# Neighbourhood attention on one core: the softmax reciprocal written 64 wide and transposed, scaling a step later, folds spread over 36 steps

## The reference

```python
# window: 8 rows x 16 columns of the token grid, clamped at the borders
s = jnp.einsum('bqhd,brqkhd->bqhrk', qi, kc) * scale + bias[None]
p = jax.nn.softmax(s.reshape(b, GRID_W, h, kh * WIN_COLS), axis=-1)
return jnp.einsum('bqhrk,brqkhd->bqhd', p, vc)
```

## Time and profile before

| | |
|---|---|
| median of 3 executions | 1835.57 us (1833.83 to 1836.62) |
| the profiled execution | 1836.12 us, its span 1834.1 us |
| granted TensorE clock, whole span | 0.984 of full speed |
| busy, share of the span | PE 97%, PEld 77%, DVE 46%, ACT 25%, POOL 28% |
| attention, 398 to 536 us: busy | PE 136.10, DVE 99.95, ACT 100.61, POOL 101.83 us |

### The profile page before, as it was taken

How to read it: one execution, slowest core, us unless ns; L and a number is a source line. 1 busy time by engine, 2 the same in 40 slices (tenths; PEclk the granted TensorE clock), 3 DMA queues, 4 the chain that set the end, 5 groups by cost and what they waited for, 6 DMA issues and landing times.

```text
span 1834.1 us, 22190 instructions
## 1 busy us (share of the span) xinstructions
PE 1779.0 (97%) x8481; PEld 1407.7 (77%) x8481; DVE 845.4 (46%) x1265; ACT 465.0 (25%) x803; POOL 521.3 (28%) x431
## 2 busy tenths in 40 slices
PE   7599999999999998899999999999999999999999
PEld 2466788877676886688888888888888888888887
DVE  2844588416876535524252615152433424252515
ACT  3533233227775004510101110111111111111010
POOL 0300122027854645005050505040312304050505
PEclk9799999999999999899999999999999999999999
DMA  9265101333323011011011110101010111101113
GB/s 344 92 195 181 37 23 35 67 73 72 76 72 136 24 35 41 17 35 35 24 35 34 34 34 15 42 23 46 23 46 23 34 34 34 34 23 34 34 34 137
DMA packets 107552, 108.70 MB, mean 59 GB/s; under 512 B 19463, under 2 KB 82145, under 8 KB 107241
## 3 DMA queue, kind: packets, MB, share of 16 engines
q1 hardware_dynamic: 106537, 104.82, 18.7%
q0 software_dynamic: 960, 3.15, 0.4%
HBM read 98.50 MB, written 9.45 MB: 59 GB/s over the span
## 4 chain that ended last, share of the span: by engine, by line
PE 75%; DVE 2%; issue 0%; ACT 0%; POOL 0%; DVEq 0%; ACTq 0%; POOLq 0%
PE banks L104 22%; PE banks L105 22%; PE banks L106 22%; PE banks L1006 2%; PE banks L1015 2%; PE banks L1345 2%; PE banks L1040 2%; PE banks L1024 1%; PE banks L992 1%; DVE h_hi L1701 0%; PE banks L1814 0%; DVE xn L1694 0%; DVE h_lo L1704 0%; PE banks L1328 0%; ACT t_second L1585 0%
## 5 line engine op out<-in xcount | busy, mean ns | idle before, releaser
L1768 POOL TENSOR_TENSOR x<-x,ff_scratch 128x512 f32<-128x512 f32 x198 | 263.4, 1364 | 834.5 <-DVE ff_scratch L1661 833.8
L104 PE MATMUL banks<-h_hi,wff_hi 128*128 128x512 f32 x1056 | 414.0, 392 | 10.9 <-POOL h_lo L1755 6.1
L105 PE MATMUL banks<-h_lo,wff_hi 128*128 128x512 f32 x1056 | 412.0, 390 | 0.0
L106 PE MATMUL banks<-h_hi,wff_lo 128*128 128x512 f32 x1056 | 411.9, 390 | 0.0
L1520 DVE TENSOR_TENSOR wff_lo<-wff_raw,wff_hi 128x1024 fp32r<-128x1024 f32 x66 | 81.5, 1235 | 404.3 <-ACT wff_hi L1516 404.3
L104 PEld LDWEIGHTS banks<-h_hi,wff_hi 128*128 128x128 f32 x1056 | 199.1, 189 | 52.0 <-issue 9.3
L106 PEld LDWEIGHTS banks<-h_hi,wff_lo 128*128 128x128 f32 x1056 | 198.9, 188 | 41.6
L105 PEld LDWEIGHTS banks<-h_lo,wff_hi 128*128 128x128 f32 x1056 | 199.1, 189 | 40.6
L1661 DVE TENSOR_TENSOR ff_scratch<-banks,gate 128x512 f32<-128x512 f32 x264 | 177.1, 687 | 71.9 <-PE banks L106 48.5
L104 PE MATMUL banks<-wff_hi,ff_hi 128*128 128x512 f32 x528 | 205.4, 389 | 0.0
L105 PE MATMUL banks<-wff_lo,ff_hi 128*128 128x512 f32 x528 | 205.4, 389 | 0.0
(11 more groups left out here) (174 smaller groups left out, 2255.3 us busy)
## 6 DMA issues: line engine op xcount, KB each, us to landing
ada_raw<-in_w_ada SPq DMA_DIRECT2D x16, 1024.0 KB, 6.6
wff_raw<-in_w_gate SPq DMA_DIRECT2D x22, 512.0 KB, 4.8
wff_raw<-in_w_up SPq DMA_DIRECT2D x22, 512.0 KB, 3.8
wff_raw<-in_w_down SPq DMA_DIRECT2D x22, 512.0 KB, 3.2
ada<-in_w_ada SPq DMA_DIRECT2D x4, 2048.0 KB, 12.3
win_raw<-in_w_in SPq DMA_DIRECT2D x16, 512.0 KB, 3.8
x_first<-in_x_sample SPq DMA_DIRECT2D x2, 2048.0 KB, 17.8
wo_raw<-in_w_o SPq DMA_DIRECT2D x4, 1024.0 KB, 5.1
```

The lines of the kernel that those rows point to most:

```text
L104: pe.matmul(out, lhs[0], rhs[0], start=start, stop=False)
L105: pe.matmul(out, lhs[0], rhs[1], start=False, stop=False)
L106: return pe.matmul(out, lhs[1], rhs[0], start=False, stop=stop)
L1768: pool.tensor_tensor(part, part, scratch[:, n % 3], ALU.add).then_inc(d_added, 1)
```

## The change

Five edits, all in the attention stage:

1. `recip` writes the reciprocal of each of the two row sums 64 times over into a new tile `recips` (128 x 128, two buffers) instead of two numbers. The input is read with a stride of 0. It also waits for the spread two units back, which frees the buffer.
2. `spread` is a single whole-array transpose of that tile instead of two matmuls.
3. On PE it stands ahead of the transposes of the probabilities and a step later: step s has spread(s-2), turn(s-1), turn_v, scores(s+1), values(s-1).
4. `copy_scale` on ACT and `scale_out` on DVE come a step later, so each engine has one more step at the end.
5. The 24 folds stand in steps 12 to 23, one in each, and in steps 24, 26, ... 46; the column copies ahead of the first fold are split in two halves (ahead of fold 0 and of fold 12).

```diff
--- before.py
+++ after.py
@@ -812,6 +812,7 @@
     s_ring = at("s_ring", [128, 2, 2, 384], F32, BASE + 57344)
     pt_ring = at("pt_ring", [128, 2, 2, 384], F32, BASE + 63488)
     stats = at("stats", [128, 3, 2 * PAIRS_A], F32, BASE + 69632)
+    recips = at("recips", [128, 2, 128], F32, BASE + 206848)
     scale_sb = at("scale_sb", [128, 2, 128], F32, BASE + 70784)
 
     bias_in, mask_in = kept.bias_in, kept.mask_in
@@ -821,7 +822,7 @@
     p_turned, pt_act, pt_dve, pv_done, scale_spread = (
         sem(n) for n in ("p_turned", "pt_act", "pt_dve", "pv_done", "scale_spread"))
     v_act, v_dve = sem("v_act"), sem("v_dve")
-    FOLD_STEP = PAIRS_A // 2
+    FOLD_STEPS = list(range(PAIRS_A // 4, PAIRS_A // 2)) + list(range(PAIRS_A // 2, PAIRS_A, 2))
     BLOCKS = FT * NB
 
     def pair_unit(w):
@@ -909,18 +910,18 @@
             act.activation(v_tok[:, NVT * b:NVT * b + 4], banks[:, 7].rearrange("p (t f) -> p t f", f=128), ACT.Copy
                            ).then_inc(v_act, 1)
         values_ready(0)
-        for s in range(PAIRS_A + 1):
+        for s in range(PAIRS_A + 2):
             if s < PAIRS_A:
                 exp(s, 0)
-            if s:
+            if 1 <= s <= PAIRS_A:
                 copy_pt(s - 1)
             if s < PAIRS_A:
                 exp(s, 1)
             m = block_at(s, 2)
             if m is not None:
                 values_ready(m)
-            if s:
-                copy_scale(s - 1)
+            if s >= 2:
+                copy_scale(s - 2)
             if s == PAIRS_A - 1:
                 mix.copy_maps(act)
 
@@ -936,7 +937,10 @@
 
         def recip(w):
             dve.wait_ge(exped, 2 * w + 2)
-            dve.reciprocal(stats[:, 2, 2 * w:2 * w + 2], stats[:, 1, 2 * w:2 * w + 2]).then_inc(recip_done, 1)
+            if w >= 2:
+                dve.wait_ge(scale_spread, w - 1)
+            dve.reciprocal(recips[:, w % 2].rearrange("p (h f) -> p h f", h=2),
+                           bass.AP(stats, 2 * PAIRS_A + 2 * w, [[6 * PAIRS_A, 128], [1, 2], [0, HEAD]])).then_inc(recip_done, 1)
 
         def copy_pt(w):
             n = pair_unit(w)[4]
@@ -964,13 +968,13 @@
         score(0, 0)
         score(0, 1)
         values_ready(0)
-        for s in range(PAIRS_A + 2):
+        for s in range(PAIRS_A + 3):
             if 1 <= s <= PAIRS_A:
                 recip(s - 1)
-            if s >= 2:
-                scale_out(s - 2)
-            if FOLD_STEP <= s < PAIRS_A:
-                mix.fold(dve, s - FOLD_STEP)
+            if s >= 3:
+                scale_out(s - 3)
+            if s in FOLD_STEPS:
+                mix.fold(dve, FOLD_STEPS.index(s))
             if 1 <= s <= PAIRS_A:
                 copy_pt(s - 1)
             if s + 1 < PAIRS_A:
@@ -1020,11 +1024,7 @@
             pe.wait_ge(recip_done, w + 1)
             if w:
                 pe.wait_ge(scale_copied, w)
-            for hh in range(2):
-                last = pe.matmul(banks[64 * hh:64 * hh + 64, 6, 0:128],
-                                 stats[:, 2, 2 * w + hh:2 * w + hh + 1].broadcast_to((128, 64)), ident[:],
-                                 start=True, stop=True)
-            last.then_inc(scale_spread, 1)
+            pe.transpose(banks[:, 6, 0:128], recips[:, w % 2], ident[:]).then_inc(scale_spread, 1)
 
         def values(w):
             p, b, c, rows, n = pair_unit(w)
@@ -1044,8 +1044,10 @@
         scores(0)
         turn_v(0, 0)
         turn_v(0, 1)
-        for s in range(PAIRS_A + 1):
-            if s:
+        for s in range(PAIRS_A + 2):
+            if s >= 2:
+                spread(s - 2)
+            if 1 <= s <= PAIRS_A:
                 turn(s - 1)
             if s == PAIRS_A - 1:
                 mix.make_maps(pe)
@@ -1055,8 +1057,7 @@
                     turn_v(m, part)
             if s + 1 < PAIRS_A:
                 scores(s + 1)
-            if s:
-                spread(s - 1)
+            if 1 <= s <= PAIRS_A:
                 values(s - 1)
 
     return Stage(run_sp, run_pool, run_act, run_dve, run_pe)
@@ -1146,10 +1147,11 @@
     def fold(dve, i):
         c, r, a, b = FOLDS[i // 2]
         t0, t, _ = REQS[r]
-        if i == 0:
+        if i in (0, len(FOLDS)):
+            groups = slice(c, c + FT // 2)
             for q, (first, length, _) in enumerate(REQS):
                 dve.wait_ge(u_in[q], 16)
-                dve.tensor_copy(uo[:, :, first // 2:first // 2 + 1], u[:, :, first:first + 1])
+                dve.tensor_copy(uo[:, groups, first // 2:first // 2 + 1], u[:, groups, first:first + 1])
         near, far = u[:, c, t0 + a:t0 + b], u[:, c, t0 + t - b + 1:t0 + t - a + 1][:, ::-1]
         if i % 2 == 0:
             dve.tensor_tensor(uo[:, c, t0 // 2 + a:t0 // 2 + b], near, far, ALU.subtract).then_inc(fold_odd, 1)
```

## The result

The changed kernel takes **1845.96 us** in the median (1841.84 to 1847.03), the kernel before 1835.57, both over five executions: +10.4 us, ratio 1.005 with a 95% interval of 1.0035 to 1.0066. The forecast was +8.7, slower with 0.78. The profiled execution has a span of 1843.9 us against 1834.1, +9.8.

A forecast was written before the change was run, and what follows sets the result against it. PE was taken to set the attention stage's pace, the change closing a PE-DVE loop with handovers: 0.1 + 4.0 + 4.9 - 0.3 = +8.7 us, giving a median of 1844.3 us, range 1837.5 to 1850.

The forecast's parts named there:

- the reciprocal: On DVE, each step: the 128-column reciprocal takes 948 ns and holds DVE 0.87 us, 0.79 more than before.
- The reading of 8 cycles a column: DVE's reciprocal at 8 cycles a column, from the skill's page: 1188 ns, 0.24 us more a step; chance 0.02.
- the zigzag without folds: Steps 0 to 11: path PE, DVE, PE plus 0.27 of handovers, 8.06 us per three steps against 8.03.
- PE's saving of 0.13 a step: On PE: one transpose replaces the spread's two matmuls, saving 0.13 us a step, between 0.11 and 0.16.
- the first twelve steps: Steps 0 to 11, no folds: 0.03 us more in each three steps, four times, +0.1 us.
- The last steps: Last two steps of the stage: no score left, DVE has room, PE's saving stays, -0.3 us.
- The later scaling: copy_scale and scale_out a step later: costs nothing; if the 2.2 us at the end did not cover it, below 1 us once.
- the mean stays my term: Folds on DVE priced at their mean, 0.49 us each; +4.0 us in steps 12 to 23, +4.9 in 24 to 46.
- the port rule: VectorE instructions with two SBUF inputs and GpSimd instructions reading SBUF exclude each other; folds' price then hangs on where POOL stands.
- the dearer folds: DVE has no idle time left, each fold meets POOL more often, up to +0.65 us each: 1848 to 1860; chance 0.13.
- The rival of hiding handovers: Handovers between PE and DVE hide; the larger of their own times bounds, 1836.8 to 1840 us; chance 0.18.
- the faster rival: Wide reciprocal costs little, up to 0.69 us; PE keeps the path and its 6.2 us: 1829.4 us; chance 0.06.

## Why the prediction was right, and where not

**Right: the reciprocal.** 948 ns expected, 945 measured, and 0.86 us of DVE instead of 0.87. The reading of 8 cycles a column is refuted with it.

**Right: the zigzag without folds.** 8.06 against 8.07 for three steps, with handovers of 0.10 and 0.18 (0.10 and 0.17 in the sum). PE's saving of 0.13 a step was 0.11: 8.03 to 7.70 for three steps where PE is the bound, in the versions with a narrow reciprocal. So the first twelve steps cost next to nothing, as expected: 0.04 us in each three. The last steps were forecast at -0.3 us and cost +0.6: from the 46th reciprocal to the Fourier part it is 8.8 us for 8.2.

**Right: nothing behind the stage.** The later scaling cost nothing. scale_out ends at 547.57, ACT reads `a_out` at 549.18. The granted clock is 1.00 from 500 to 535 us, as before, and 0.98 over the whole stage in both.

**The wrong step: "The 24 folds sum to ... 13.6 us, 0.57 each, less 0.08 of overlap: 0.49", and "the mean stays my term".** A fold has no price of its own. It holds DVE 0.33 us when POOL is idle and up to 1.16 behind a pair of masks. The traces settle how much: in all 14 of them, for all 336 folds, the record is 0.41 us long, or, where a POOL instruction was running when the fold started, what was left of that instruction and 0.28 us more, whichever is longer, to within 0.02 us. It holds behind masks and behind POOL's copy of the values alike. In the fold step shown, 451.40 - 450.76 + 0.28 = 0.92. In the changed kernel the holds repeat as 0.37, 0.84, 0.64, and the two on the path are the dear ones: 2.79 + (2.44 + 0.84) + (2.49 + 0.64) + 0.27 = 9.47, the measured number, where the sum had 9.03. With every second step a fold 9.2 and 8.6 were measured, 8.92 in the mean, for 8.65. That is 4 x 0.44 + 8 x 0.27 = 3.9 us, which takes the forecast of 8.7 to 12.6; the 42 steps show 12.5, and the median of the runs, with its other clocks, 10.4. That the median came so near to 8.7 is in part luck: the stage itself grew by 12.9 us, and 2.4 us of that came back behind it with the clock. DVE's busy time in the stage is 133.20 us, where 137 was named. The prediction had named the port rule beside this term and the dearer folds as a rival of 0.13. What it missed is that the wide reciprocal itself moves the fold behind the gap in POOL's pair: the term depended on the other term.

The rival of hiding handovers is refuted by the rows at 422.48 and 425.09. The turning point named for the faster rival, a reciprocal of 0.69 us, was not tried by itself; with the reciprocal of 32 columns the ratio is 1.0000, as the place and the folds still cost what the transposes bring.

## What to carry to other kernels

When an engine on the path is relieved by giving work to another, count that engine's step with its handovers, not its busy share: here DVE had 38 us of idle time, was given 38, and the loop between the two engines closed. An instruction of one shape whose duration differs from row to row may be waiting inside its own record, as the folds did; find out for what (here another engine's instruction, not its own shape) before its mean goes into a sum. And an instruction that stands between the two ends of a handover is cover: removing it from there can cost what it took.

## What the runs showed of the hardware

That VectorE and POOL exclude each other at one SBUF port was foreseen as a possibility, not that it would be this sharp. A fold of 255 or 256 columns holds DVE 0.33 us alone. It holds it 0.64 in the kernel before, where it waits for the first mask of a pair and gets in ahead of the second, 0.84 and 0.64 in the changed kernel, where it waits for the end of the pair, and 1.16 when the second mask has just begun; none of the 336 folds ended within a POOL instruction that had begun before it. The other way round, a fold that starts 0.16 us ahead of a long mask takes its usual time, and the mask takes 1.12 us for 1.00. POOL's records are rough at their ends, so the 0.2 us or so around them are not to be read closely. The Trainium skill's page "SBUF — State Buffer" (section "Who interferes with whom") says that whichever instruction starts first has the port for its whole length; all of these rows agree. The copy of two numbers to 128 columns, from SBUF to SBUF, was held as well, 0.51 us where it takes 0.23. The 128-column reciprocal was not: it takes 935 to 954 ns beside POOL or alone.
